# Large tiles of a hybrid DeltaNet and MoBA block moved to starts at multiples of 2 KB of a partition

## What is computed

```python
h = rms_norm(x, norm_pre_w)
proj = jnp.einsum('bsd,df->bsf', h, w_in)          # 1024 x 10256
qkv_a, z_a, beta_a, dec_a, qkv_b, z_b, gate_logits = jnp.split(proj, cuts, axis=-1)
...
oa = gated_delta_rule(qa, ka, va, g, beta)         # 8 heads of 128
ya = rms_norm(oa, dn_onorm_w) * silu(z_a)
ob = moba_attention(qb, kb, vb, rel_bias)          # one causal block of 256 keys, T5 bias
yb = ob * silu(z_b)
merged = gates[:, :, 0] * (ya @ w_branch[0]) + gates[:, :, 1] * (yb @ w_branch[1])
out = x + rms_norm(merged @ w_out, norm_post_w)
```

## The kernel before, in words

| tile | size in a partition | before | changed |
|---|---|---|---|
| raw, w_hi, w_lo (slots of 4 KB) | 16 KB each | 128 | 0 |
| h_hi, h_lo | 8 KB each | 1856 | 0 |
| y_hi, y_lo | 16 KB each | 576 | 0 |
| xin, cst | 8 KB, 1.5 KB | 128 | 0 |
| bias | 8 KB | 1856 | 704 |
| gt, wbd2 | 768 B, 1 KB | 64, 640 | 128, 896 |
| acc, act, bT, kT_all, th_E, vtok_all, sub, pt, y32 and others behind `power` | | as before | the same remainders, 32 KB further on |

## Time and profile before

### The profile page before, as it was taken

The page is one execution under the profiler, slowest core; times in us unless marked ns, Lnnn a source line. Parts: engine busy times, 40 slices in busy tenths (PEclk is TensorE's granted clock), DMA queues, the critical chain, the costliest instruction groups (busy, mean ns, idle before and its releaser), DMA issues.

```text
span 355.8 us, 6674 instructions
## 1 busy us (share of the span) xinstructions
PE 347.6 (98%) x2387; PEld 318.4 (89%) x2387; DVE 270.0 (76%) x551; ACT 218.8 (62%) x483; POOL 58.7 (16%) x114
## 2 busy tenths in 40 slices
PE   7999999999999999999999999999999999999993
PEld 5889998888899999999999999999998888888882
DVE  3869897599997868978788797878977656566744
ACT  5877894542457667686867766777676544425421
POOL 1534436500050000301103020030301101000011
PEclk9999999999999999999999999999999999999999
DMA  8667948793698485446745565465534735766423
GB/s 264 178 193 194 334 158 270 198 329 119 167 257 228 121 214 141 121 122 164 188 120 128 145 178 147 120 164 145 165 121 138 247 118 172 254 226 236 124 113 118
DMA packets 76206, 63.48 MB, mean 178 GB/s; under 512 B 4724, under 2 KB 62478, under 8 KB 76174
## 3 DMA queue, kind: packets, MB, share of 16 engines
q1 hardware_dynamic: 73838, 59.37, 57.3%
q0 software_dynamic: 1152, 3.30, 3.1%
q10 hardware_dynamic: 1184, 0.39, 0.5%
HBM read 61.46 MB, written 1.59 MB: 177 GB/s over the span
## 4 chain that ended last, share of the span: by engine, by line
PE 84%; DVE 8%; DMA 3%; issue 2%; ACT 1%; POOL 0%; DVEq 0%; SPq 0%; ACTq 0%; POOLq 0%
PE banks L1395 40%; PE banks L1450 15%; PE banks L1657 6%; PE banks L1413 6%; DVE w_lo L919 3%; DVE sub L1061 2%; DMA xin<-in_x_dram 1%; DMA raw<-in_w_in_dram 1%; DMA sub<-m_blocks 1%; PE banks L1545 1%; PE banks L1523 1%; PE banks L1562 1%; PE banks L1551 1%; PE banks L1380 1%; DVE sub L1063 1%
## 5 line engine op out<-in xcount | busy, mean ns | idle before, releaser
L919 DVE TENSOR_TENSOR w_lo<-raw,w_hi 128x1024 fp32r<-128x1024 f32 x102 | 123.8, 1220 | 42.3 <-ACT w_hi L670 41.6
L670 ACT CAST w_hi<-raw 128x1024 fp32r<-128x1024 f32 x103 | 107.2, 1047 | 30.0 <-PE banks L1450 12.3
L1395 PE MATMUL banks<-h_hi,w_hi 128*128 128x256 f32 x440 | 64.0, 288 | 0.2 <-DVE acc L989 0.2
L1395 PE MATMUL banks<-h_lo,w_hi 128*128 128x256 f32 x440 | 59.4, 277 | 0.0
L1395 PE MATMUL banks<-h_hi,w_lo 128*128 128x256 f32 x440 | 59.3, 277 | 0.0
L1395 PEld LDWEIGHTS banks<-h_hi,w_hi 128*128 128x128 f32 x440 | 55.2, 189 | 0.7 <-DVE acc L989 0.3
L1395 PEld LDWEIGHTS banks<-h_hi,w_lo 128*128 128x128 f32 x440 | 54.2, 188 | 0.0
L1395 PEld LDWEIGHTS banks<-h_lo,w_hi 128*128 128x128 f32 x440 | 54.2, 188 | 0.0
L989 DVE SCALAR_TENSOR_TENSOR acc<-banks,vec,acc 128x255 f32<-128x255 f32 (+2 forms) x72 | 34.5, 480 | 3.7 <-ACT acc L790 1.5
L616 POOL TENSOR_TENSOR so<-so,rnq 128x2 f32<-128x2 f32 x8 | 2.0, 251 | 162.8 <-ACT junk L857 162.8
L790 ACT ACTIVATE acc<-banks,vec 128x256 f32<-128x256 f32 x16 | 7.6, 473 | 17.4 <-PE banks L1395 17.4
(11 more groups left out here) (258 smaller groups left out, 607.6 us busy)
## 6 DMA issues: line engine op xcount, KB each, us to landing
raw<-in_w_in_dram SPq DMA_DIRECT2D x80, 512.0 KB, 4.9
raw<-in_w_branch_dram SPq DMA_DIRECT2D x16, 512.0 KB, 4.7
raw<-in_w_out_dram SPq DMA_DIRECT2D x8, 512.0 KB, 4.2
xin<-in_x_dram SPq DMA_DIRECT2D x2, 512.0 KB, 3.8
th_E<-g_rows POOLq DMA_DIRECT2D x2, 512.0 KB, 7.2
bias<-bias_rows POOLq DMA_DIRECT2D x1, 1024.0 KB, 7.5
raw<-in_x_dram SPq DMA_DIRECT2D x2, 512.0 KB, 3.7
out_dram<-xin SPq DMA_DIRECT2D x4, 256.0 KB, 2.0
```

Of the source, the lines that this page charges most:

```text
L670: nc.scalar.copy(w_hi[:, t % SLOTS, :], raw[:, t % SLOTS, :]).then_inc(s_hi, 1)
L919: v.tensor_tensor(w_lo[:, t % SLOTS, cols], raw[:, t % SLOTS, cols], w_hi[:, t % SLOTS, cols].bitcast(F32), ALU.subtract).then_inc(s_lo, 1)
L1395: last = mm(ps, w, r, start=part == 0 and k == 0, stop=part == 2 and k == KT - 1)
```

## The change

Four small tables (`gt`, `wbd2`, `ssqk`, `ng`; together 1,920 bytes of a partition) are declared first, and fill the space up to the next multiple of 2 KB. Behind them come `raw`, `w_hi`, `w_lo`, `h_hi`, `h_lo`, `y_hi` and `y_lo`, and then the rest in its old order. No instruction is added, removed or moved on any engine: the sequences of the two programs are the same row by row, waits included. Only addresses differ.

```diff
+        gt = sb("gt", [P, 12, NC, HEADS])
+        wbd2 = sb("wbd2", [P, KT, 4 * HEADS], F32R)
+        ssqk = sb("ssqk", [P, NC, HEADS])
+        ng = sb("ng", [P, NC, HEADS])
         raw = sb("raw", [P, SLOTS, D])
         w_hi = sb("w_hi", [P, SLOTS, D], F32R)
         w_lo = sb("w_lo", [P, SLOTS, D], F32R)
+        h_hi = sb("h_hi", [P, KT, SEQ], F32R)
+        h_lo = sb("h_lo", [P, KT, SEQ], F32R)
+        y_hi = sb("y_hi", [P, 2, HEADS, SEQ], F32R)
+        y_lo = sb("y_lo", [P, 2, HEADS, SEQ], F32R)
         xin = sb("xin", [P, NC, D])
...
         wbd = sb("wbd", [P, KT, 2 * HEADS])
-        wbd2 = sb("wbd2", [P, KT, 4 * HEADS], F32R)
...
-        h_hi = sb("h_hi", [P, KT, SEQ], F32R)
-        h_lo = sb("h_lo", [P, KT, SEQ], F32R)
         bias = sb("bias", [P, HEADS, SEQ])
...
-        gt = sb("gt", [P, 12, NC, HEADS])
         tab = sb("tab", [P, 11, HEADS])
-        ng = sb("ng", [P, NC, HEADS])
         grow = sb("grow", [HEADS, SEQ])
-        ssqk = sb("ssqk", [P, NC, HEADS])
...
-        y_hi = sb("y_hi", [P, 2, HEADS, SEQ], F32R)
-        y_lo = sb("y_lo", [P, 2, HEADS, SEQ], F32R)
```

## The result

The change made the kernel slower: 363.18 us (four runs, 362.94 to 363.31) against 357.60 us (four runs), ratio 1.0155, 95% interval 1.0137 to 1.0173. That is 5.6 us more. The profiled execution has a span of 361.3 us, 5.5 more than before.

A forecast was written before the change was run, and what follows sets the result against it. TensorE's matmul pace was taken to bound the kernel; matmul reads, weight loads, ScalarE and VectorE work and DMA were each priced at 0 on a profiled 357.55 us, giving 357.6 us, with a range of 350.0 to 360.0.

The forecast's parts named there:

- What bounds the kernel: Whole kernel: TensorE never stands still for another engine, so time is the number of matmuls times their pace.
- the price of 0 ns for a matmul's two reads: TensorE float32r matmuls: new tile starts change nothing in their reads, 0 ns per matmul.
- Weight loads: TensorE's loads of weights: one in four crosses a 2 KB boundary before, none after; priced at 0.
- Does it come from where they begin?: Float32r matmuls: whether their surplus over the clock's pace, 12.3 us at most, comes from tile starts; answered no.
- All three comparisons: Trace before: 2 KB crossings, finer start units and plain float32 operands, each said to show no cost of a start.
- 114 throughout: 256-column matmuls: one pace of 114 ns (229 for 512 columns) in stretches of very different ScalarE and VectorE load.
- 0.445 ns per column: Float32r streams of 512 and 256 columns: called the same loss per column despite different tile starts.
- lie on a straight line: ScalarE cast and VectorE subtraction: two sizes at different remainders fit whole clocks per column, so nothing to win.
- Two reads meet: Every float32r matmul: equal remainders make readers collide, up to 3 ns each, 5.8 us slower, 363.4 us; chance 0.14.
- The 3 ns: Bound on the slowdown per float32r matmul, from the spread of plain float32 records, 275 against 272 ns.
- The rivals on the fast side: Float32r matmuls: a 2 KB crossing (0.10), a small part of it (0.08) or a finer start unit (0.03); together 0.21.
- Crossing a boundary: Matmul reads: each 2 KB crossing costs at most 6 ns, gain 7.5 us, 350.1 us; chance 0.10, small part 0.08.

The follow-up runs named there:

- g4_before_h0: Kernel before the change with only h_hi and h_lo 320 bytes further on, at the weight tiles' remainder (128): 363.89 us, ratio 1.0170.
- e2_all64: Changed kernel with raw, w_hi, w_lo, h and y all 64 bytes further on, distances between them kept: 363.44 us, ratio 1.0161.
- e1_h64: Changed kernel with the h and y tiles 64 bytes further on, weight tiles left in place: 361.52 us, ratio 1.0107.
- e4_h128: Changed kernel with the h and y tiles 128 bytes further on, weight tiles left at 0: 364.63 us, ratio 1.0195.

## Why the prediction was wrong

**What bounds the kernel** was right: TensorE's pace is the time, it waits for no one, and so a few nanoseconds a matmul would be seen at once. ScalarE, VectorE and the DMAs do as little as I had them do.

**The failed step is the price of 0 ns for a matmul's two reads**: "I price the edit at 0 ns per matmul", and "Weight loads ... Priced at 0". I asked of each read alone whether it crosses a boundary, and not what the moving read and the weight load meet in each other. The runs put +6.3 us there (in g4_before_h0 +6.9), with matmuls that went from 113.8 to 120.0 ns apart and records of loads that went from 188 to 192. Which of the two reads is held up is not shown: at distance 128 the pace is 118.7 ns and the loads take 189.

**"Does it come from where they begin?"** was answered rightly for the question put, and the question was too narrow. All three comparisons look at one operand's start. They rule out a cost of crossing 2 KB and a cost of a start's own alignment, and e2_all64 confirms both: at remainder 64 the wide reads cross again, and their pace is 227.5 ns against 227.8. None of them can see the distance between two operands, for in the kernel before each pairing of tiles occurs at one distance only (192 by 512 for the 256-column form, 320 and 64 for the wide one). A trace in which a quantity never varies says nothing on it.

**Three readings of the trace before were too quick.** The paces are not "114 throughout": the same chain has tiles of 2.83 us (129.60 us, above), and 12 of the 110 thirds lo x hi and hi x lo run at 118 ns, so something in the place or order of things already set a pace. The 0.445 ns per column is the whole pace and not a loss. And the two sizes of the cast and of the subtraction "lie on a straight line" because two points always do; that their starts cost nothing was shown only by the changed kernel, where they take 1046 and 1222 ns.

**The rival "Two reads meet" is what happened.** Its sign and its time (363.4 against 363.18) were right, its mechanism only in part. It had every float32r matmul longer by the same amount, most where ScalarE and VectorE are busiest. In truth it is 6 ns on 1360 matmuls and -1.3 on 576, with ScalarE and VectorE busy or idle. The 3 ns were taken from 275 against 272 ns of plain float32 records, a spread that is the same before and after (275 against 273), so it measured no meeting. That the two errors cancel is luck. I gave the rival 0.14 because the pace doesn't change with the load of ScalarE and VectorE. That is true after the change as well, and speaks only against a meeting with those engines. It says nothing of a meeting of TensorE's two reads with each other, which run side by side in every stretch. On this the Trainium skill, page TensorE: Matmul & The Clock Gate, section "Step-by-step: what each phase is for", says that loading the next weights doesn't steal read bandwidth from the running matmul. The traces of this case don't bear that out for float32r: the pace is 113.8 or 120.0 ns by the distance of the two alone. Whether it is bandwidth that is lost, no run here shows.

**The rivals on the fast side** had 0.21. Crossing a boundary is worth nothing in either form. The wide form did get 1.3 ns faster, but by the distance 0: in e1_h64 and e4_h128, with the weight tiles at a multiple of 2 KB all the same, it is 3.6 and 4.9 ns slower than before. The range of 350 to 360 was laid towards the side on which I had the larger bounds, and cut the dear half of the rival that speaks for slower; with a mechanism that can touch all matmuls and no row that bounds it, both ends should have stood.

## What to carry to other kernels

Where TensorE streams float32r without a gap, the place of a tile is part of the speed. What counts first is the start of the moving tile against that of the stationary one, here modulo 512 bytes or a divisor of it. Giving everything the same round start was the dearest choice tried for the 256-column form (120 against 113.8 ns), and the best of those tried for the wide one (227.8 against 229.1), so the mix of forms decides. After any change to the list of tiles, even of one that is small, compare the pace from start to start of the main matmul lines with the one before, and tile by tile, for a mean can hide two paces. When arguing from a trace that an address costs nothing, list first which distances occur in it at all.

## What the runs showed of the hardware that was not expected

- Two operands at equal remainders are dear in one form and cheap in the other: 120.0 against 113.8 ns for 256 columns, 227.8 against 229.1 for 512. With h 64 or 128 bytes from w the wide form loses 3.6 and 4.9 ns.
- At a good distance a stream still has two paces, 113 to 114 and 118 ns, and most tiles keep one to their end. Which it is hangs on where the weight tiles lie and where `cst` and `xin` do: 59 of 104 thirds or 7, with `h` at the same distance from the weights. Where `h` lies, at 192 or 448, made no difference.
- Plain float32 products took the same time before and after: the records of 256 columns of L1551 and L1562 380 ns, with 217 ns from start to start. Their operands kept their distances from each other in all runs, apart from `cst` against `act` (109 ns a transpose with `cst` at 0 and at 128), so this doesn't show that such products are free of the effect.
- Why 512 bytes (or 256), and which part of the memory or of TensorE the two reads share, was not settled. The map at odd multiples of 32 bytes is not explained by one distance, either.
